# Norms turned in two halves of the tokens, attention by single steps, and earlier slab splits in a two-block fp32 kernel

## What is computed

```
block 1: u = rms_norm(x) @ w_in                       # 1024 x 7864: mla | fox | ssm | gates
         y_a = mla(u)     # 8 heads, key chunks of 64 allowed up to the query's chunk
         y_b = fox(u)     # 8 heads of 64, causal, with decay F
         y_c = ssm(u)     # conv, state-space scan, gated norm (z)
         x += (sum of sigmoid(gate_n) * (y_n @ w_br_n)) @ w_out
         x += (silu(conv(rms_norm(x) @ w_up)) * conv(...)) @ w_down      # d_ff 2816
block 2: xn = rms_norm(x); proj = xn @ w_in_2
         spatial gating (su, sv), gated linear attention, band attention (8 heads of 64),
         conformer conv (31 taps)
         x += (sum of gated branches) @ w_out_2
         x += relu(rms_norm(x) @ w_ff1)^2 @ w_ff2               # d_ff 4096
         x += sigmoid(rms_norm(x) @ w_ple_gate + b) * (p @ w_ple)
         out = rms_norm(x)
rms_norm(x) = x * rsqrt(mean(x*x) + 1e-6) * gain
attention: softmax(q k^T * scale + mask) v, per head, in query tiles of 128
```

## Time and profile before

| what | value |
|---|---|
| median of 3 runs | 2110.9 us (2108.1 to 2115.18) |
| the profiled execution | 2110.22 us, its span 2108.5 us |
| mean granted TensorE clock | 0.987 |
| PE / DVE / ACT / POOL busy | 96% / 54% / 37% / 4% |
| chain that ended last | PE 90%, DVE 5%, ACT 3%, POOL 2%, issue 1% |
| HBM traffic | 180.81 MB read, 87 GB/s over the span |

### The profile page before, as it was taken

The page is one execution under the profiler, slowest core; times in us unless marked ns, Lnnn a source line. Parts: engine busy times, 40 slices in busy tenths (PEclk is TensorE's granted clock), DMA queues, the critical chain, the costliest instruction groups (busy, mean ns, idle before and its releaser), DMA issues.

```text
span 2108.5 us, 23431 instructions
## 1 busy us (share of the span) xinstructions
PE 2032.5 (96%) x9653; PEld 1664.2 (79%) x9653; DVE 1139.7 (54%) x1616; ACT 785.8 (37%) x1068; POOL 84.3 (4%) x102
## 2 busy tenths in 40 slices
PE   7999899999999999999999899999999999999995
PEld 6886678878888788888878687888888788888874
DVE  5756547477544676357368777743435443234245
ACT  5546543344422433133232534542233333133132
POOL 0003300110000000000000200000000000000000
PEclk9999999999999999999999999999999999999998
DMA  4320022211422233333333122223232222332231
GB/s 129 100 81 20 2 94 86 80 60 61 140 88 92 80 100 100 96 86 88 110 120 100 41 77 94 80 81 100 100 100 83 86 93 100 100 100 95 86 114 55
DMA packets 164440, 184.44 MB, mean 87 GB/s; under 512 B 6759, under 2 KB 125798, under 8 KB 164334
## 3 DMA queue, kind: packets, MB, share of 16 engines
q1 hardware_dynamic: 160718, 173.98, 26.0%
q10 hardware_dynamic: 2912, 6.83, 0.9%
q0 software_dynamic: 704, 2.13, 0.3%
HBM read 180.81 MB, written 2.12 MB: 87 GB/s over the span
## 4 chain that ended last, share of the span: by engine, by line
PE 90%; DVE 5%; ACT 3%; POOL 2%; issue 1%; DMA 0%; SPq 0%; DVEq 0%; POOLq 0%; ACTq 0%
PE ps L432 27%; PE ps L434 27%; PE ps L433 27%; PE ps L549 1%; ACT arena L1247 1%; PE ps L564 1%; PE ps L535 1%; POOL arena L1178 1%; PE ps L746 1%; PE ps L516 1%; DVE arena L2474 1%; PE ps L773 1%; POOL X L1178 1%; PE ps L594 1%; DVE X L2277 0%
## 5 line engine op out<-in xcount | busy, mean ns | idle before, releaser
L1728 DVE TENSOR_TENSOR WL<-W,WH 128x2048 fp32r<-128x2048 f32 (+1 forms) x166 | 375.3, 2261 | 362.1 <-ACT WH L1222 354.2
L432 PE MATMUL ps<-HH,WH 128*128 128x512 f32 x1400 | 549.4, 392 | 7.1 <-DVE HL L1751 4.4
L434 PE MATMUL ps<-HH,WL 128*128 128x512 f32 x1400 | 545.9, 390 | 0.0
L433 PE MATMUL ps<-HL,WH 128*128 128x512 f32 x1400 | 545.9, 390 | 0.0
L1222 ACT ACTIVATE WH<-W 128x2048 fp32r<-128x2048 f32 (+1 forms) x166 | 313.2, 1888 | 290.6 <-DMA W<-in_w_ff_dram 121.5
L432 PEld LDWEIGHTS ps<-HH,WH 128*128 128x128 f32 x1400 | 263.2, 188 | 65.3 <-issue 6.6
L434 PEld LDWEIGHTS ps<-HH,WL 128*128 128x128 f32 x1400 | 263.2, 188 | 55.1
L433 PEld LDWEIGHTS ps<-HL,WH 128*128 128x128 f32 x1400 | 263.2, 188 | 53.8 <-issue 0.2
L432 PE MATMUL ps<-WH,arena_r 128*128 128x512 f32 (+1 forms) x616 | 239.7, 389 | 1.6 <-issue 1.6
L433 PE MATMUL ps<-WL,arena_r 128*128 128x512 f32 (+1 forms) x616 | 239.2, 388 | 0.0
L434 PE MATMUL ps<-WH,arena_r 128*128 128x512 f32 (+1 forms) x616 | 239.1, 388 | 0.0
(11 more groups left out here) (339 smaller groups left out, 2243.2 us busy)
## 6 DMA issues: line engine op xcount, KB each, us to landing
W<-in_w_in_dram SPq DMA_DIRECT2D x50, 1024.0 KB, 5.2
W<-in_w_ff_dram SPq DMA_DIRECT2D x32, 1024.0 KB, 5.2
W<-in_ffn_w_up_dram SPq DMA_DIRECT2D x44, 512.0 KB, 5.0
W<-in_w_gate_dram SPq DMA_DIRECT2D x16, 1024.0 KB, 4.9
W<-in_ffn_w_down_dram SPq DMA_DIRECT2D x10, 1024.0 KB, 5.0
W<-in_w_out_dram SPq DMA_DIRECT2D x8, 1024.0 KB, 5.0
W<-in_w_branch_dram SPq DMA_DIRECT2D x8, 1024.0 KB, 5.0
W<-in_w_br_ssm_dram SPq DMA_DIRECT2D x4, 1024.0 KB, 5.0
```

Of the source, the lines that this page charges most:

```text
L432: pe.matmul(out_, st[0], mv[0], start=first, stop=False)
L433: pe.matmul(out_, st[0], mv[1], start=False, stop=False)
L434: return pe.matmul(out_, st[1], mv[0], start=False, stop=last)
L1728: dve.tensor_tensor(WL[:, j % RING, 0:n], W[:, j % RING, 0:n], plain(WH[:, j % RING, 0:n]), ALU.subtract).then_inc(slab_lo, 1)
```

## The change

1. Norms n1 to n5 go in two halves of 256 tokens. `norm_half(half)` transposes two token tiles into 4 banks (two k side by side in a bank); ScalarE (`evict`) and VectorE (`lows`) take 256 columns at a time. The first half is turned when tiles 0 and 1 are scaled. On VectorE `lows(0)` stands between the last add and the scaling of tile 3, on ScalarE `evict(0)` before tile 3's square. Both then split the slab after next, and take the second half.
2. The first slab of the next gemm is multiplied half by half (`gemm_f_by_halves`, k outside, the two 128-feature blocks inside), with the transposes of the second half between. Before the ple gemm the second half is turned after token tile 1.
3. In front VectorE scales the rows first and copies the parameters behind them, and the first slab is split in four pieces, VectorE following ScalarE piece by piece.
4. Attention goes step by step: scores of step s, turn of s-3, and at odd s the outputs of s-5 and s-4. VectorE takes reciprocals per step, GpSimd scales per step. Outputs of all pairs use bank 7; bank 6 joins the ring. Slabs that fall into attention are split in four pieces over four steps, a fox head's Q and K are turned in two steps.
5. The third slab of z is split first in the ssm stage; 12 taps move into band's steps, and a split of su comes 12 taps earlier.

The diff, cut to its core (of long functions that are replaced, only the new lines stand):

```diff
...
-PAIR_BANKS = (6, 7)
+PAIR_BANK = 7
+LAG = 3
...
+    def normed(k, half):
+        tag, n, seen = norm_now
+        while seen[half] <= k:
+            if seen[half] % 2 == 0:
+                pe.wait_ge(norm_low, KT * n + KT // 2 * half + seen[half] // 2 + 1)
+            else:
+                taken(pe, (tag, half, seen[half] // 2))
+            seen[half] += 1
+    norm_now = [None, 0, [KT, KT]]
     def hn(k):
-        normed(k)
+        normed(k, 0)
+        normed(k, 1)
     def hnt(k, t):
-        normed(k)
+        normed(k, t // 2)
+    def gemm_f_by_halves(name, w, tiles):
+        banks = [bank((name, c), counted=False) for c in range(tiles)]
+        for half in range(2):
+            if half == 1:
+                norm_half(1)
+            cols = slice(half * S // 2, (half + 1) * S // 2)
+            for k in range(KT):
+                normed(k, half)
+                for c in range(tiles):
+                    mm = product(banks[c][:, cols], [x[:, k, c * P:(c + 1) * P] for x in w],
+                                 [HH[:, k, cols], HL[:, k, cols]], k == 0, k == KT - 1)
+                    if half == 1 and k == KT - 1:
+                        mm.then_inc(pe_done, 1)
+                        DONE[name, c] = len(DONE) + 1
...
     def norm(tag, n):
+        norm_now[:] = [tag, n, [0, 0]]
+        norm_half(0)
+    def norm_half(half):
+        tag, n, _ = norm_now
+        pe.wait_ge(xn_ready, NT * n + 2 * half + 2)
+        for i in range(KT // 2):
+            b = bank((tag, half, i))
+            for k in (2 * i, 2 * i + 1):
+                for t in range(2):
+                    tr = pe.transpose(b[:, (k % 2) * 2 * P + t * P:(k % 2) * 2 * P + (t + 1) * P],
+                                      at(XN, NT, DM)[:, 2 * half + t, k * P:(k + 1) * P], ident[:, :])
+            tr.then_inc(pe_done, 1)
+    def attention(tags, first, lhs, rhs, v, p, pts, ready, beside_scores=None):
+        ring[:] = [b for b in ring if b != PAIR_BANK]
+        steps = len(tags) * STEPS
...
+        def outputs(step):
+            ...
+            if t == 0:
+                outs[0] = bank((tag, "O", pair), counted=False, pinned=PAIR_BANK)
...
+        for step in range(steps):
+            scores(step)
+            if step >= LAG:
+                turns(step - LAG)
+            if step >= LAG + 2 and step % 2 == 1:
+                outputs(step - LAG - 2)
+                outputs(step - LAG - 1)
             if beside_scores is not None:
+                beside_scores(step)
+        turns(steps - LAG)
         def last_steps(t):
             if t == 0:
+                turns(steps - 2)
+                outputs(steps - 4)
+                outputs(steps - 3)
             if t == 1:
+                turns(steps - 1)
             if t == 2:
+                outputs(steps - 2)
+                outputs(steps - 1)
...
-            gemm_f("c", w, KT, 0, 2, hn, 2 * i)
+            if i == 0:
+                gemm_f_by_halves("c", w, 2)
+            else:
+                gemm_f("c", w, KT, 0, 2, hn, 2 * i)
...
-        def turn_fox(d):
-            h = d - 2
+        def turn_fox(step):
+            h, keys = divmod(step - NT, 2)
-                turn_head("fox", "QT", h, Qf, 66)
-                turn_head("fox", "KT", h, Kf, 66)
+                if keys:
+                    turn_head("fox", "KT", h, Kf, 66)
+                else:
+                    turn_head("fox", "QT", h, Qf, 66)
...
-        ring.append(PAIR_BANKS[0])
...
-            gemm_f(("f1", i), w, KT, 0, 2, hn)
+            if i == 0:
+                gemm_f_by_halves(("f1", i), w, 2)
+            else:
+                gemm_f(("f1", i), w, KT, 0, 2, hn)
-            gemm_t_long("pg", A["w_ple_gate_2"][0].rearrange("(k p) n -> p k n", p=P), 512 * half, hnt, half)
+            gemm_t_long("pg", A["w_ple_gate_2"][0].rearrange("(k p) n -> p k n", p=P), 512 * half, hnt, half,
+                        between=(lambda t: norm_half(1) if t == 1 else None) if half == 0 else None)
...
-        attention(0, STEPS, heads_p())
+        attention(0, 2 * STEPS, heads_p())
...
-    def attention(first_double, doubles, p):
-        for d in range(doubles):
-            pool.wait_ge(sums_inverted, first_double + d + 1)
-            for j in (2 * d, 2 * d + 1):
-                s = 2 * (j % STEPS) + 1
-                pool.tensor_scalar(weights(p, s), weights(p, s), rowinv[:, s:s + 1], None, ALU.mult)\
-                    .then_inc(odd_weights_ready, 1)
+    def attention(first, steps, p):
+        for step in range(steps):
+            pool.wait_ge(sums_inverted, first + step + 1)
+            s = 2 * (step % STEPS) + 1
+            pool.tensor_scalar(weights(p, s), weights(p, s), rowinv[:, s:s + 1], None, ALU.mult)\
+                .then_inc(odd_weights_ready, 1)
...
+    def split_piece(j, q):
+        assert made[0] == j
+        n = slabs[j][0] * slabs[j][1] // 4
+        sl = slice(q * n, q * n + n)
+        act.wait_ge(slab_in[j % RING], 16 * loaded(j))
+        ins = act.activation(WH[:, j % RING, sl], W[:, j % RING, sl], ACT.Copy)
+        if q < 3:
+            ins.then_inc(slab_piece, 1)
+        else:
+            ins.then_inc(slab_hi, 1)
+            made[0] += 1
...
+        def evict(half):
+            cols = slice(half * S // 2, (half + 1) * S // 2)
+            for k in range(KT):
+                b = use(act, (f"n{n + 1}", half, k // 2))
+                act.activation(HH[:, k, cols], b[:, k % 2 * 256:k % 2 * 256 + 256], ACT.Copy,
+                               scale=pcol(gain, k)).then_inc(hi_ready, 1)
+        if tag is None:
+            for t in range(NT):
                 act.wait_ge(x_in[t], 16)
+                square(t)
+            for q in range(4):
+                split_piece(0, q)
+            taken(act, ("par", 0))
+            evict(0)
+            evict(1)
+            return
+        act_only_splits(tag)
+        for t in range(NT):
+            if t == NT - 1:
+                evict(0)
+            taken(act, (tag, t, 1))
             square(t)
+        split(slab_of[tag, 0, 1] + 2)
+        evict(1)
...
+        steps = len(tags) * STEPS
+        for now in range(steps + LAG):
+            if now < steps:
+                tag, j, pair, t = step_of(tags, now)
+                for s in (2 * j, 2 * j + 1):
+                    taken(act, (tag, "S", s))
+                    act.activation(weights(p, s), weights(p, s), ACT.Exp, bias=rowneg[:, s:s + 1],
+                                   scale=-1.0, accum_out=rowsum[:, s:s + 1]).then_inc(probs_ready, 1)
+            step = now - LAG
+            tag, j, pair, t = step_of(tags, step)
+            if step >= 0 and t >= 2:
                 ...
             if beside_scores is not None:
+                beside_scores(now)
...
-        def beside_scores(d):
-            if 0 <= d - 2 < HEADS:
-                act_turn_head("fox", d - 2, at(15360, HEADS, S), 66, 2)
-            if d == 10:
-                split(slab_of["z", 0, 0] - 1)
-            if d == 13:
-                split(slab_of["z", 0, 0])
+        def beside_scores(step):
+            h, keys = divmod(step - NT, 2)
+            if 0 <= h < HEADS and not keys:
+                act_turn_head("fox", h, at(15360, HEADS, S), 66, 2)
+            if 24 <= step < 28:
+                split_piece(slab_of["z", 0, 0], step % 4)
...
-        def beside_scores(d):
-            if d == 4:
-                split(slab_of["sv", 0, 0])
+        def beside_scores(step):
+            if 8 <= step < 12:
+                split_piece(slab_of["sv", 0, 0], step % 4)
...
+    pieces = [0]
+    def split_piece(j, q, high_made=False):
+        assert made[0] == j
+        n = slabs[j][0] * slabs[j][1] // 4
+        sl = slice(q * n, q * n + n)
+        if q < 3 and not high_made:
+            pieces[0] += 1
+            dve.wait_ge(slab_piece, pieces[0])
+        else:
+            dve.wait_ge(slab_hi, j + 1)
+        ins = dve.tensor_tensor(WL[:, j % RING, sl], W[:, j % RING, sl], plain(WH[:, j % RING, sl]),
+                                ALU.subtract)
+        if q == 3:
+            ins.then_inc(slab_lo, 1)
+            made[0] += 1
...
-        b = use(dve, ("par", 0))
-        freed(dve.tensor_copy(par[:, 0:P], b[:, 0:P]), ("par", 0))
...
+        def lows(half):
+            cols = slice(half * S // 2, (half + 1) * S // 2)
+            for k in range(KT):
+                name = (f"n{n + 1}", half, k // 2)
+                if k % 2 == 0:
+                    high()
+                    high()
+                ins = dve.scalar_tensor_tensor(
+                    HL[:, k, cols], ps[HOME[name][0]][:, k % 2 * 256:k % 2 * 256 + 256], pcol(gain, k),
+                    plain(HH[:, k, cols]), ALU.mult, ALU.subtract)
+                if k % 2 == 0:
+                    ins.then_inc(norm_low, 1)
+                else:
+                    freed(ins, name)
+        def made(t):
+            scaled(t, n, at(XN, NT, DM)[:, t, :]).then_inc(xn_ready, 1)
         if tag is None:
```

(92 more changed lines are left out.)

183 lines of the change are left out of this document (44 added, 139 removed).

## The result

The changed kernel takes 2099.4 us (median of 4 runs, 2095.2 to 2101.0) against 2111.2 (2108.1 to 2115.2): ratio 0.9945, 95% interval [0.9928, 0.9961]. It is faster by 11.8 us where 24.4 were forecast.

The account below looks back on a forecast made before the run. TensorE was busy 96% of the span, so only its idle and slow pieces could be won. Gains 9+2+6.2+0.8+5+1.4 = 24.4 us from 2110.9 gave 2086.5 us; own range 2078 to 2095, with middle rivals 2076 to 2104.

Parts of the forecast that it names:

- The pace of 256 columns: In the half-slab gemms: one 256-column product every 0.12 us, bounds 0.107 and 0.227, so 5.8 us for a half.
- The norms: Norms n2 to n5 behind a gemm: gains 4.3, 3.0, 1.7, 2.4, less 2.5 for fallen clocks; -9 us (-2 to -13).
- The front's first slab: Front (n1): first product at 16.2 instead of 20.47, both halves done at 31.4 instead of 33.3; -2 us (0 to -5).
- z's third slab: Start of the ssm stage: splitting it first removes a 3.46 us wait and some slow clock; -5 us (-3 to -6).
- the wait before the outputs: Attention: TensorE waits for VectorE's copy out of the one output bank, 0.5 to 1.8 us per pair.
- su: Twelve conv taps moved into the last attention steps make su's second slab ready earlier; -1.4 us (0 to -3).
- The pieces of the two slabs cost 0.6 and 1.1 instead of 0.2 and 3.7: Attention, mla and fox: slabs split in pieces, copy's 2.6 us wait included, give -2.2 of the stage's -6.2 us.
- With pieces at 1.1: Band: pairs of 9.6 us against some 9.3 without a split, slab pieces costing 1.1; -0.8 us (-4 to +5).
- My bound of +6: Attention's slow limit: each hand-over costs 0.1 us more and the copy queues behind a piece; +6 instead of -6.2 us.
- the list of what would show me wrong: Halves' products every 0.19 or 0.227; fox pairs 11 us or more; over 0.5 between halves; 0.50 clock over 4 us per norm.
- both blocks of the split gemm finish together, so their evictions bunch, and the next slab has 10.9 us of products as cover.: Split gemm behind a norm: bunched evictions lie beside the next slab's products; forecast 0 for the second slab.
- attention pays: Rival: one output bank and six hand-overs per step cost 1.2 us more for each of twelve pairs; 2101 us, chance 0.18.

Follow-up runs that it names:

- the whole-slab kernel: Changed kernel with z's first slab and sv's split whole, without pieces, ScalarE at step 24 (8), VectorE two steps later: 2083.1 us.
- the last kernel: Changed kernel with pieces two steps apart, parameter transposes inside second slab, norm low parts before tile 2's scaling and before slab split, outputs copied first: 2068.1 us.

## Why the prediction was wrong

**Right.** The pace of 256 columns (0.12), the low parts (3.22/8 = 0.40) and high parts (3.02/8 = 0.38). The norms: 8.9 against 9. n2 4.1 for 4.3; n3 and n4 lost 1.5 us each to the half clock, where I had given back 2.5 in all; n5 3.5 for 2.4. The front's first slab: first product 16.02 for 16.2, the second half done at 31.3 for 31.4. Its -1.8 for -2 is in part luck: kernels with the same front have -0.1 to -1.9 in their profiles, and the kernel with z's and su's edits alone, whose front is the old one, has -1.6. z's third slab 5.4 for 5. The pairs ahead of the pieces that cost: fox 10.0 with VectorE's pieces of the slab before in it (9.75 and 0.6 for them), mla 11.3 for 11.5, band 10.0 for 9.6, the wait before the outputs 0.2 to 0.65. (In the layout of a pair TensorE's terms add up to 6.9 at turn 2 and not to 7.2; its wait of "0.5 to 0.8" covers both.)

**Wrong.** In the profiled executions 14.3 us are missing: 7.8 and 4.2 in the two attention parts and 4.2 at the second slab, less 1.9 that su gave beyond its forecast. The steps that failed:

1. *"The pieces of the two slabs cost 0.6 and 1.1 instead of 0.2 and 3.7"* and *"With pieces at 1.1"* in band. I priced a piece by its duration and not by what VectorE waits for in front of it. ScalarE's piece stands behind the same step's exponentials and two copies, VectorE's piece is at the end of VectorE's step, and VectorE gets there up to 1.9 us earlier. Behind it the next scores' minima were held (they start at 226.69, right behind the piece), though the scores were there; then the exponentials, the turn, and the output copy followed late. The Trainium skill says in "Perfetto Trace Analysis", Tensor Engine Instruction (MATMUL, LD_WEIGHTS), that ScalarE and VectorE queues are strictly first in, first out. By this rule the minima could not pass the waiting piece, and the trace agrees. My bound of +6 named a copy that queues behind a piece, but gave it no price, and the list of what would show me wrong had such a wait only for the norm halves. It cost 10.2 us in fox and 7.1 in band: the term came out at +1.6 and +3.4 for -6.2 and -0.8, and without the wait it is -8.6 and -3.7, better than forecast.
2. *"both blocks of the split gemm finish together, so their evictions bunch, and the next slab has 10.9 us of products as cover."* So it is in n2 to n4, not in the front, where something that needs banks stands ahead of the cover. It cost 4.2 us where I had 0, and all of it came back when the taker of banks was moved.

The other way round, su gave 3.3 for 1.4: its wait of 1.4 went, and behind it the half clock was shorter, as the mean over like stretches of 9 us tells (0.62 before, 0.81 after). That second 1.6 is the clock's and not the edit's: it was 0.0 in the whole-slab kernel, where the half clock lasted 6.8 us as before, and 3.2 in the last kernel, where the clock did not fall at all.

**The rival "attention pays"** gave 2101 and the time is 2099.4, but its mechanism is not what happened. It had 1.2 us in each of twelve pairs from the one bank and the hand-overs; measured are 12.0 us over the forecast, nearly all from the pieces' waits on and nearly none in the pairs ahead. That its number is the measured one is luck. The bank's 2.2 us waits are for the most part a consequence: they fell to 0.2 in that pair when the pieces were moved, with the bank as it was.

**Size of the clock's part.** Four kernels have the same attention code up to z: the changed one, that with later parameters and the two with other norm orders. All have the waits of 0.9, 0.6 and 2.2 us in the last pair. In two the half clock lasted 13.7 us and attention came to +1.6 and +1.5; in the two others 6.8 us, and -1.3 and -1.4. So 6.9 us more at 0.50 cost 2.9 us, and of the 10.2 us in fox some 5.7 are the clock (estimate, 13.7 x 2.9/6.9), the rest idle time. Why it stays down longer once and not the other time is open.

## What to carry to other kernels

A piece of work that two engines share, one behind the other, cost most here when it stood at the same place of both in-order queues: give the second engine its part one step later, and read in the first one's queue what stands ahead. Price an inserted instruction by the wait in front of it as well as by its duration, and the wait by what is queued behind it. When work is regrouped so that two banks come free together, look for the next taker of banks, not only for the next consumer of the data.

## What was not expected of the hardware

The same waits were followed by 6.8 to 13.7 us at half clock, which is 3 us of time between kernels that differ elsewhere; a single profile of one of them misjudges the stage by that much. At su one and the same edit shows as 1.7, 3.3 or 4.9 us, by whether 6.8, 3.4 or 0 us of half clock follow. Doubling the weight loads in a slab (48 to 96, each with half the columns) cost some 0.8 us per slab at full clock: in n2 the two halves take 5.83 and 5.86 us from first to last start, 11.7 together, against 48 x 0.227 = 10.9.
